# A last step of its own for the experts, a first small unit taken from the plan, and both directions of a recurrence in one block

## The reference, cut to what matters

```python
logits = xt @ w_router + b_router
top_logits, top_idx = lax.top_k(logits, TOP_K)          # 4 of 32
...
gate, up = jnp.split(xb @ w_gu[e] + b_gu[e], 2, axis=-1)  # 1024 -> 2048
gate = jnp.minimum(gate, SWIGLU_LIMIT)
up = jnp.clip(up, -SWIGLU_LIMIT, SWIGLU_LIMIT)
act = (up + 1) * (gate * jax.nn.sigmoid(SWIGLU_ALPHA * gate))
return act @ w_dn[e] + b_dn[e]                            # 1024 -> 1024
```

```python
for d, f_raw in enumerate((f_fwd, f_bwd)):
    ...
    y = y + hgrn2_direction(qh, log_f, kh, vh)   # d == 1: on flipped sequences, flipped back
```

## Time and profile before

| what | value |
|---|---|
| time of three runs, us | 3672.73, 3675.73, 3681.72 (median 3675.73) |
| the profiled execution's own time, us | 3674.47 |
| its span in the trace, us | 3672.7 |
| granted TensorE clock, mean | 0.952 |
| PE busy | 3399.4 us, 93% of the span |
| VectorE busy | 1599.3 us, 44% |
| ScalarE busy | 772.6 us, 21% |

### The profile page before, as it was taken

How to read it: one execution, slowest core, us unless ns; L and a number is a source line. 1 busy time by engine, 2 the same in 40 slices (tenths; PEclk the granted TensorE clock), 3 DMA queues, 4 the chain that set the end, 5 groups by cost and what they waited for, 6 DMA issues and landing times. The chain is left out here.

```text
span 3672.7 us, 35084 instructions
## 1 busy us (share of the span) xinstructions
PE 3399.4 (93%) x12610; PEld 1909.9 (52%) x12610; DVE 1599.3 (44%) x2814; ACT 772.6 (21%) x1570; POOL 266.8 (7%) x373
## 2 busy tenths in 40 slices
PE   8995689999988899999999999698999989989998
PEld 3443338444554344444444444235544589768886
DVE  6883725983353111111111111466526288644554
ACT  2103211122121101101101001225444256220001
POOL 1000021000001000000000000100000187000000
PEclk9995699999998999999999999799999999999999
DMA  8860037211136999999999996513323110312220
GB/s 267 291 207 30 7 149 280 72 69 66 69 124 250 406 404 389 399 404 385 401 396 395 400 393 250 201 47 93 119 93 113 35 30 30 137 51 88 92 92 24
DMA packets 209097, 711.44 MB, mean 194 GB/s; under 512 B 16198, under 2 KB 27544, under 8 KB 174156
## 3 DMA queue, kind: packets, MB, share of 16 engines
q1 hardware_dynamic: 183436, 633.45, 45.7%
q0 software_dynamic: 14576, 48.71, 3.8%
q10 hardware_dynamic: 10960, 27.63, 2.0%
HBM read 655.86 MB, written 53.89 MB: 193 GB/s over the span
## 5 line engine op out<-in xcount | busy, mean ns | idle before, releaser
L2533 PE MATMUL bank<-moe_gu,all_hT 128*128 128x512 f32 x1088 | 469.9, 592 | 3.1 <-PEq L2201 1.9
L2730 DVE TENSOR_SCALAR all_hT<-bank 128x512 f32<-128x512 f32 x51 | 35.3, 691 | 813.9 <-PE bank L2539 668.3
L2533 PEld LDWEIGHTS bank<-moe_gu,all_hT 128*128 128x128 f32 x1088 | 206.6, 190 | 262.9 <-issue 261.5
L2553 PE MATMUL bank<-moe_gu,all_hT 128*64 128x512 f32 x1088 | 238.2, 596 | 1.5 <-DVE all_hT L2731 1.5
L2573 PE MATMUL bank<-moe_dn,moe_rows 128*128 128x512 f32 x512 | 224.0, 595 | 3.9 <-ACT moe_rows L2652 3.9
L1919 PE MATMUL bank<-all_hT,early_w 128*128 128x512 f32 x512 | 220.2, 592 | 0.0
L2553 PEld LDWEIGHTS bank<-moe_gu,all_hT 128*64 128x64 f32 x1088 | 80.8, 138 | 156.0 <-issue 153.7
L1919 PEld LDWEIGHTS bank<-all_hT,early_w 128*128 128x128 f32 x512 | 97.3, 190 | 122.0 <-issue 122.0
L2573 PEld LDWEIGHTS bank<-moe_dn,moe_rows 128*128 128x128 f32 x512 | 96.0, 190 | 122.5 <-issue 114.8
L1981 DVE SCALAR_TENSOR_TENSOR b_conv<-conv_ya,all_table,b_conv 128x512 f32<-128x512 f32 x240 | 159.4, 744 | 0.0
L3750 PE MATMUL bank<-hg_qs,hg_ks 128*128 128x64 f32 x896 | 118.1, 285 | 25.1 <-ACT hg_ks L3653 14.0
(11 more groups left out here) (779 smaller groups left out, 5424.1 us busy)
## 6 DMA issues: line engine op xcount, KB each, us to landing
moe_gu<-in_w_gu_dram SPq DMA_DIRECT2D x136, 2048.0 KB, 14.4
moe_dn<-in_w_dn_dram SPq DMA_DIRECT2D x68, 2048.0 KB, 13.9
early_w<-in_w_in_dram SPq DMA_DIRECT2D x13, 2048.0 KB, 9.1
expert_rows<-b_z POOLq DMA_DIRECT2D x49, 512.0 KB, 20.3
mods_w<-in_w_mod_dram SPq DMA_DIRECT2D x48, 512.0 KB, 5.3
mods_w<-in_ada_w_dram SPq DMA_DIRECT2D x48, 512.0 KB, 4.9
late_w<-in_w_up_dram SPq DMA_DIRECT2D x8, 2048.0 KB, 9.0
late_w<-in_w_down_dram SPq DMA_DIRECT2D x8, 2048.0 KB, 7.7
```

What stands on the lines that cost most here:

```text
L2533: mm = nc.tensor.matmul(B[bank][:], xb2[:, k, :], gu[:, q, kk, col:col + HALF], start=(k == 0), stop=False)
L2553: mm = nc.tensor.matmul(B[bank][part, :], xb1[:, k % 4, k // 4, :], gu[:, 4 + q, kk, col + h * HALF:col + (h + 1) * HALF], start=(k == 0), ...
L2730: vec.tensor_scalar(g, gate[:], SWIGLU_LIMIT, None, ALU.min).then_inc(clipped, 1)
```

## The change

Experts. The plan names one expert with at most 32 rows beyond its big units ("spill"); these rows no longer count as a small unit. The big unit of that expert (or of another, where there is none) is put into the last step. That step, written out after the loop, runs the big unit, the spilled 32 rows with the same weights (`gate_up3`, `down3`: the 1024 columns of an output in four quarters of 256, each quarter in 32 output partitions of its own: 64 products and 8 with the bias in `gate_up3`, 32 in `down3`), and the last small unit with its down products (`late_dn`, loaded into the place of used gate weights). The first small unit is the first of the plan instead of expert 1: its gate-up weights are loaded when the list of units is known, and its rows are picked by PE between the second and third quarter of the first `gate_up2` (`pick_first`). The first half of expert 0's `dn` is loaded earlier, once the norm's scratch is free. `expert_blocks` has 42 named semaphores instead of 25, and `sems` now also clears ahead of a call with 38 or more names.

Recurrence. One block runs 16 passes (`PASSES`), the 8 heads forward and then the 8 heads backward. Masks are halved in width and both loaded at the start; `A` is cleared again for passes 8 and 9, `S` for pass 8. The 1 MB load `first_out` is issued at pass 10 instead of at the end.

With the counts above the plan goes as follows. Before: 15 big units; 19 small ones (17 smaller experts, the one row left of expert 16, and expert 1's); two small ones become big: 17 and 17, so 17 steps. After: 15 big and 17 small, expert 16's one row is the spill, one small one becomes big: 16 and 16; expert 16's big unit goes to the last step, so 15 steps and the last one, 16 in all.

```diff
 def sems(nc, ctx, *names):
-    if len(USED) > 80:
+    if len(USED) > 80 or USED and len(names) >= 38:
         clear_used(nc, USED)
...
+SPILL, SPILL_AT = 32, SMALL_AT + (MAX_STEPS + 1) * SMALL
...
 def route(...):
-            pe.wait_ge(first_known, 2 * TT)
+            pe.wait_ge(first_known, TT)
             for k in range(KT):
                 for t in range(TT):
-                    mm = nc.tensor.matmul(B[4 + k // 2][:, (k % 2) * 256:(k % 2) * 256 + P + SMALL],
-                                          htm[:, t, k * P:(k + 1) * P], first_rows[:, t, :], start=(t == 0),
+                    mm = nc.tensor.matmul(B[4 + k // 2][:, (k % 2) * 256:(k % 2) * 256 + P],
+                                          htm[:, t, k * P:(k + 1) * P], first_rows[:, t, 0:P], start=(t == 0),
...
-            after(nc.vector.memset(n_small[:, 1:2], 1.0))
+            after(tt(passed[:], n_e[:], split[:], ALU.subtract))
+            after(tt(spill[:], n_small[:], n_big[:], ALU.min))
+            after(nc.vector.scalar_tensor_tensor(out=spill[:], in0=passed[:], scalar=float(SPILL), in1=spill[:],
+                                                 op0=ALU.is_le, op1=ALU.mult))
...
+            after(tt(n_lead[:], n_big[:], tail[:], ALU.subtract))
...
+            after(nc.vector.tensor_scalar(last[:], upto_small[:, NE - 1:NE], -1.0, None, ALU.add))
+            after(tt(last[:], last[:], upto_big[:, NE - 1:NE], ALU.max))
...
+            for t in range(TT):
+                after(nc.vector.tensor_scalar(first_rows[:, t, P:], slot[:, 0:SMALL], beyond[:, t, :], None, ALU.is_equal))
...
 def expert_blocks(...):
-            load_dn(0, 0, None, (0,))
             load_gu(0, 0, range(3))
             sp.wait_ge(core.rows_placed, placed)
+            sp.wait_ge(first_picked, 1)
...
+            sp.wait_ge(rows2_loaded, 16 * last + 16)
+            for g in range(4):
+                sp.dma_start(rows3[quarter(g), :], rows_dram[SPILL_AT:SPILL_AT + SPILL, g * QUARTER:(g + 1) * QUARTER]).then_inc(
+                    rows3_loaded, 16)
             load_dn(0, last, 2 * last)
-            load_dn(1, last, 2 * last + 1)
+            e = expert_of(sp, 1, last)
+            for c in range(2):
+                sp.wait_ge(gu_used[0][c], last + 2)
+                sp.dma_start(late_dn[:, c].rearrange("p (k n) -> p k n", n=D), dn_v[
+                    bass.ds(e, 1), :, 4 * c:4 * c + 4, :].rearrange("a p k n -> (a p) k n")).then_inc(late_loaded, 16)
...
+            def pick_first():
+                chosen = first_choice(spare)
+                for k in range(KT):
+                    for t in range(TT):
+                        mm = nc.tensor.matmul(B[7][:, k * C:(k + 1) * C], htm[:, t, k * P:(k + 1) * P], chosen[:, t, P:],
+                                              start=(t == 0), stop=(t == TT - 1), skip_group_check=True)
+                mm.then_inc(first_picked, 1)
...
+            def gate_up3():
+                left = by_quarter(xb3)
+                pe.wait_ge(xb3_made, 1)
+                for k in range(KT):
+                    for x in range(2):
+                        for g in range(4):
+                            mm = nc.tensor.matmul(B[(7, 1)[x]][quarter(g), 0:QUARTER], left[:, k % 2, k // 2, :],
+                                                  gu[:, k // 2, k % 2, x * E + g * QUARTER:x * E + (g + 1) * QUARTER],
+                                                  start=(k == 0), stop=False, skip_group_check=True)
...
-            n = count(pe)
-            with pe.Fori(2, n) as i:
+            last = last_of(pe)
+            with pe.Fori(2, last) as i:
                 step_units(i, False)
-            turn_hid1(n)
-            down1(n, last_of(pe))
+            gate_up2(last, False)
+            pe.wait_ge(rows3_loaded, 64)
+            turn3(rows3, 5, rows3_turned)
+            turn_hid1(last)
+            down1(last, before_last(pe))
+            pe.wait_ge(read_out, 3 * last + 1)
+            gate_up3()
+            turn_hid2(last, True)
+            down2(last, False)
+            pe.wait_ge(hid3_made, 1)
+            pe.wait_ge(hidT2_made, 2 * last + 2)
+            turn3(hid3, 5, hid3_turned)
+            pe.wait_ge(yb1_made, last)
+            down3()
+            pe.wait_ge(read_out3, 1)
+            gate_up1(last, False)
+            turn_hid1(last + 1, True)
+            down1(last + 1, None, True)
...
 def experts(...):
-                for x in range(2):
-                    for q in range(4):
-                        sp.dma_start(gu[:, 4 * x + q], weights[2][x, :, 2 * q:2 * q + 2, :]).then_inc(gu_loaded[x][q], 16)
+                for q in range(4):
+                    sp.dma_start(gu[:, q], weights[2][0, :, 2 * q:2 * q + 2, :]).then_inc(gu_loaded[0][q], 16)
+                scratch_free()
+                sp.dma_start(dn[:, 0].rearrange("p (k n) -> p k n", n=D), weights[3][0, :, 0:4, :]).then_inc(dn_loaded[0], 16)
+                listed()
+                e = sp.value_load(unit_expert[1][0:1, 0:1], min_val=0, max_val=N_EXPERTS - 1)
+                for q in range(4):
+                    sp.dma_start(gu[:, 4 + q], weights[2][bass.ds(e, 1), :, 2 * q:2 * q + 2, :].rearrange(
+                        "a p k n -> (a p) k n")).then_inc(gu_loaded[1][q], 16)
...
-def hgrn_direction(core, d, q, G, K, total, v_tm, y, ident, kept_dram, ahead):
+def hgrn_recurrence(core, q, sums, keys, totals, v_tm, y, ident, kept_dram, ahead):
...
-            for h in range(HG_H):
+            for h in range(PASSES):
...
+                if h in (HG_H, HG_H + 1) and j == 0:
+                    vec.memset(A[:, h % 2, :], 0.0).then_inc(started, 1)
...
+                if h == HG_H:
+                    dve.wait_ge(out_made, h)
+                    vec.memset(S[:, order[0], :], 0.0).then_inc(cleared, 1)
...
-                    for d in range(2):
-                        hgrn_direction(core, d, hq, f[d], K[d], total[d], v_tm, hT, ident, a["y_dram"],
-                                       first_out if d else None)
+                    hgrn_recurrence(core, hq, f, K, total, v_tm, hT, ident, a["y_dram"], first_out)
```

More of the change, by code:

```diff
@@ L2185, in second_block, with route @@
     experts(core, a, xT, hT, ident, ones, mod, c)
-def route(core, spare, hT, ident, ones, gate, loaded, rows_dram, row, weight, share, unit_expert, n_steps,
+def route(core, spare, hT, ident, ones, gate, loaded, rows_dram, row, weight, share, unit_expert, last_step,
           normed, loads):
@@ L2202, in route @@
         (fold, lg, top, gt, eq, rank, need, ex, tot, n_e, n_big, n_small, upto_big, upto_small,
-         big_at, small_at, split, passed, more, expert, size) = bufs(
+         big_at, small_at, split, passed, more, expert, size, spill, tail, n_lead, shift, last, tail_expert) = bufs(
             nc, ctx, "route", fold=[P, NE], lg=SH, top=[P, TT, 8], gt=SH, eq=SH,
@@ L2221, in _ @@
         def _(sp):
-            loads(sp)
+            loads(sp, lambda: normed[-1].wait(sp, KT - 1), lambda: sp.wait_ge(steps_known, 4))
         @block.gpsimd
@@ L2404, in place_tables, with expert_blocks @@
     return (*(tables[:, n] for n in range(4)), chosen_row)
-def expert_blocks(core, weights, spare, ident, ones, b_gu, unit_expert, n_steps, rows_dram, row, weight, share):
+def expert_blocks(core, weights, spare, ident, ones, b_gu, unit_expert, last_step, rows_dram, row, weight, share):
     nc = core.nc
@@ L2525, in gate_up2 @@
                 for q in range(4):
+                    if first and q == 2:
+                        pick_first()
                     pe.wait_ge(gu_loaded[0][q], 16 * i + 16)
@@ L2543, in gate_up1 @@
             def gate_up1(i, first):
-                if not first:
+                if first:
+                    pe.wait_ge(first_made, 1)
+                else:
                     pe.wait_ge(xb1_made, i)
@@ L2576, in down2, with down1 @@
                     mm.then_inc(dn_used[c], 1)
-            def down1(done, before):
+            def down1(done, before, tail=False):
                 pe.wait_ge(hidT1_made, done)
@@ L3534, in hgrn_direction @@
     NM = NL + 1
-    order = list(range(TT)) if d == 0 else list(range(TT))[::-1]
+    orders = (list(range(TT)), list(range(TT))[::-1])
+    PASSES = 2 * HG_H
     R = 4
@@ L3607, in _ @@
         def _(act):
-            nc.scalar.activation(dec[:], total[:], ACT.Exp).then_inc(decayed, 1)
+            for d in range(2):
+                nc.scalar.activation(dec[:, d], totals[d][:], ACT.Exp).then_inc(decayed, 1)
             def turned_out(h):
@@ L3614, in ends @@
             def ends(h):
+                d, head = divmod(h, HG_H)
                 act.wait_ge(end_diffed, h + 1)
@@ L3768, in _ @@
             pe.wait_ge(zeroed, 1)
-            for h in range(HG_H):
+            for h in range(PASSES):
+                head = h % HG_H
                 for i in range(NL):
```

319 lines of the change are left out of this document (223 added, 96 removed), and 2 rows, old and new, of the table dn_used.

## The result

The changed kernel takes 3617.62 us (median of three runs, 3613.67 to 3621.61) against 3675.73: a ratio of 0.984, with a 95% interval of 0.9823 to 0.9858. The forecast was 3619. The profiled execution has a span of 3619.4 us and a time of its own of 3621.61.

The account below looks back on a forecast made before the run. PE was taken to bound steady expert steps, transfers close behind; the scatter step 0's end. From 3674.47 us, 50.6 less 7 for the later start, 1.0 and 10.5 make 55.1: 3619.4 us; forecast 3610 to 3628, range 3608 to 3634.

Parts of the forecast that it names:

- One step less, the pitch unchanged: Expert steps: 16 instead of 17, with starts of gate_up2 still 67.5 us apart.
- The last step, 100.7 us: From step 15's start to the end of down1: 100.7 us instead of 151.3, 50.6 less.
- the quarters: Last step's narrow products in four output quarters: 75 ns per instruction, 10.8 us for gate_up3.
- the rival's 54: Last step's narrow products: four-fold overlap gives 54 ns per 256-column instruction, total 3615 us; chance 0.20.
- the 83 ns pair: Smallest load-and-product pair found in the old trace, 83 ns, held against four-fold overlap in the last step.
- the last hidden chain: Last small unit in the last step: its hidden chain has nothing to hide behind, 3.5 us.
- Experts start 2.0 us later: Before step 0: SyncE's wait for the list, four loads and a semaphore clear delay the experts by 2.0 us.
- Step 1 starts 7 us later: Step 0 to step 1: moved weight loads delay the scatter only partly, 7 us taken between 3.0 and 17.3.
- the prediction's upper bound: Step 1's start: 15.3 us for 6.3 MB more beside the scatter, with the 2.0 us, gives 17.3 us.
- Rival 2: Start of the steps: the 15.3 us of transfers show in full, at scatter or steps 1 to 3, 3630; chance 0.13.
- Clear: Semaphore clear ahead of combine moves to the experts' start: 1.0 us less behind the experts.
- The recurrence: Both directions in one block, the ninth head following at the steady pitch: 10.5 us gained, bounds 9 and 11.5.

Follow-up runs that it names:

- e4: Changed kernel with pick_first making only the last of its eight column groups, so the first small unit's inputs are incomplete: 3615.65 us, ratio 0.9845.
- e1: Kernel before with only the recurrence's two directions joined in one block and the masks halved: 3661.21 us, ratio 0.9955.
- e9: Changed kernel with VectorE's two list casts moved earlier and step 1's first three gate-up quarters loaded behind the scatter: 3610.03 us, ratio 0.9828.
- e5: Changed kernel with step 1's first three gate-up quarters loaded behind the scatter instead of beside it: 3615.05 us, ratio 0.9839.

## Why the prediction was right

- **One step less, the pitch unchanged:** right (67.63 us, then 67.52).
- **The last step, 100.7 us:** 96.6 measured, 4.1 less. The term that was mis-sized is the quarters: 7.6 us with the bias (2227.34 less 2219.70) where 10.8 was taken. They run four at once, 55 ns each, the rival's 54; the 83 ns pair, taken as the counter-evidence, said nothing about this form. `down3` was 5.3 instead of 4.8, at a granted clock of 0.68; at 1.00 it takes 3.7. The prediction has no term for the clock there, and the 96.6 us are one of eleven profiles between 94.7 and 99.7. The waits I had set by the nearest rows were close: 3.40 us for the last hidden chain (3.5), 2.39 ahead of `down3` (2.9), 8.61 for `down1` (9.0).
- **Experts start 2.0 us later:** right (+37.96 against +35.99), and by the way that was worked out: with the 4.0 us that this execution is late taken off, SyncE's four issues end at 1146.5 (1148.34 + 2.15 - 4.0; 1146.7 forecast). The pick of 128 columns took 9.80 us, not 8.5 (by its columns it would have been 8.8), and nothing waited for it.
- **Step 1 starts 7 us later:** 11.2 measured. This is the step that failed, in the sentence "only a part of the bytes can be ahead of it": the packet counts show that all 6.3 MB go ahead of the scatter's end, 15.3 us at 413 GB/s; of these some 4 us are saved, since the weights' first issue (1148.34) comes 5 us ahead of the scatter's (1153.42) into idle engines. The 2.0 us by which step 0 is later don't come on top, as they do in the prediction's upper bound, since the scatter's end goes by the bytes. Rival 2 had the mechanism for this term, without those 4 us. That PE's pick is covered was right (e4), as long as the scatter ends last.
- **Clear:** the gap ahead of the combine shrank by 1.3 us (1.0).
- **The recurrence:** 10.5 us, the number forecast, but partly by luck. The clearing costs less than was taken (0.25 us in the two passes' pitch), e1 alone gains 11.7, and a semaphore clear that lands behind the recurrence takes 1.2 of that back.

With the measured terms the sum is -54.8 + 11.2 - 1.3 - 10.5 = -55.4 us, against the forecast's -55.1. That the total was so close is luck: two errors of 4 us cancel, a last step that was priced too dear and a start priced too cheap, and each of the two measured terms varies by about as much between profiles. The spans differ by 53.3: 4.0 us were lost ahead of the experts, which is variation, and some 2 gained behind the recurrence. Of these 2 us 1.2 are the semaphore clear: before, it stood there at 3233 us, where PE's wait has gone from 5.58 to 4.36 us; now it stands right behind the recurrence.

## What to carry to other kernels

When a load moves into a stretch where another queue's transfers are waited for, count the packets of both: as long as the engines take turns by packet, the queue with more packets left ends last, behind all bytes of the other. Here the scatter had 2304 small packets beside 1904 larger ones of the weights. Put off only what is not needed soon, and move the issue to where the engines idle, which may mean reordering a chain on another engine that the issue waits for. For a few rows beside a large unit, spread the output over four quarters and let consecutive products go to different ones.

## What the runs showed of the hardware that I had not expected

- Two queues with work share by packets, 377 to 377 in 10 us, and so by bytes 2.84 to 1.40 MB.
- Products with 32-wide weights in four output quarters run four at once in float32: 55 ns for each instruction of 256 columns, 172 when one quarter's follow one another. The Trainium skill's page "TensorEngine Tiling (Array Packing)", section "Performance Considerations", gives this four-fold tiling for a left side of 32; the trace agrees.
- The same 64 instructions behind the same wait of 2.0 us (`down3`) take 5.35 us at a granted clock of 0.68 in the changed kernel's profile and 3.66 us at 1.00 in e9's. The time of one and the same step therefore varies between executions.
- Around a wait of 9.42 us at the experts' start the granted clock is 0.63 over 14 us, a mean of the levels 2.4 and 1.2 GHz, and half of `gate_up2` takes 16.66 us instead of 13.95. Here the scatter's wait hides it; in e5 the 32 instructions behind a wait of 7.26 us took 2.3 us longer, and nothing hid that.
